# A two-layer decoder kernel: another PSUM bank for one tile, high passes of a pair ahead of low ones, and weight splits of two units at other steps

## What is computed

```python
h = rms_norm(x, norm_w[i])
proj = h @ w_in                      # layer 0: q, kc, vc, ks, vs, kw, vw, gates, z
# layer 0: rope on q, ks, kw; compressed, selected and window branches
o = g0 * o_cmp + g1 * o_sel + g2 * o_win
x = x + (o * silu(z)) @ w_out
# layer 1: q, f, i, z = split(h @ w_in); chunkwise gated recurrence
o = o * rsqrt(mean(o * o) + eps)     # per head, then g_norm
x = x + (o * silu(z)) @ w_out
```

## Time and profile before

| | us |
|---|---|
| median of 3 runs | 330.6 |
| lowest and highest | 330.0, 330.66 |
| the profiled execution | 330.72 |
| its span, first to last instruction | 328.9 |

### The profile page before, as it was taken

How to read it: one execution, slowest core, us unless ns; L and a number is a source line. 1 busy time by engine, 2 the same in 40 slices (tenths; PEclk the granted TensorE clock), 3 DMA queues, 4 the chain that set the end, 5 groups by cost and what they waited for, 6 DMA issues and landing times.

```text
span 328.9 us, 6172 instructions
## 1 busy us (share of the span) xinstructions
PE 317.3 (96%) x2380; PEld 268.4 (82%) x2380; DVE 228.9 (70%) x400; ACT 188.6 (57%) x400; POOL 57.8 (18%) x55
## 2 busy tenths in 40 slices
PE   7999999999999999999999999999999999998993
PEld 5889778867989877777678878999999788897882
DVE  2789953649569978879828726277449988489824
ACT  4694355356696666668536706838345036898223
POOL 1004022070423443346300010100000011101000
PEclk9999999999999999999999999999999999999998
DMA  7999999806390920033270773653662424001011
GB/s 229 394 335 209 265 358 195 264 31 223 105 186 0 212 47 2 0 112 146 68 253 0 257 258 127 248 201 91 227 249 91 168 96 165 2 1 66 0 64 64
DMA packets 28828, 49.41 MB, mean 150 GB/s; under 512 B 3256, under 2 KB 7744, under 8 KB 28800
## 3 DMA queue, kind: packets, MB, share of 16 engines
q1 hardware_dynamic: 25760, 44.30, 42.9%
q10 hardware_dynamic: 2528, 2.69, 4.2%
q0 software_dynamic: 512, 2.03, 1.9%
HBM read 47.97 MB, written 1.05 MB: 149 GB/s over the span
## 4 chain that ended last, share of the span: by engine, by line
PE 66%; DVE 16%; ACT 5%; issue 2%; POOL 2%; ACTq 0%; DVEq 0%; POOLq 0%
PE bank L548 61%; DVE w_lo L1073 6%; ACT w_hi L826 3%; PE bank L727 3%; DVE nmax L1268 2%; POOL rp L1427 1%; PE bank L648 1%; DVE prob_t L1280 1%; DVE qk L1357 1%; DVE ft L1324 1%; DVE qk L1343 1%; PE bank L592 1%; DVE zT L1215 1%; DVE zT L1216 0%; ACT prob L946 0%
## 5 line engine op out<-in xcount | busy, mean ns | idle before, releaser
L1073 DVE TENSOR_TENSOR w_lo<-raw,w_hi 128x1024 fp32r<-128x1024 f32 (+1 forms) x80 | 89.2, 1159 | 34.8 <-ACT w_hi L826 34.7
L548 PE MATMUL bank<-w_hi,h_hi 128*128 128x512 f32 x192 | 77.9, 412 | 2.4 <-DVE h_lo L1172 1.1
L548 PE MATMUL bank<-w_hi,h_lo 128*128 128x512 f32 x192 | 75.2, 392 | 0.0
L548 PE MATMUL bank<-w_lo,h_hi 128*128 128x512 f32 x192 | 75.2, 392 | 0.0
L826 ACT ACTIVATE w_hi<-raw 128x1024 fp32r<-128x1024 f32 (+1 forms) x80 | 72.9, 967 | 2.1 <-issue 1.9
L548 PE MATMUL bank<-h_hi,w_hi 128*128 128x256 f32 x224 | 64.9, 290 | 0.1
L548 PE MATMUL bank<-h_hi,w_lo 128*128 128x256 f32 x224 | 63.5, 283 | 0.0
L548 PE MATMUL bank<-h_lo,w_hi 128*128 128x256 f32 x224 | 63.5, 283 | 0.0
L548 PEld LDWEIGHTS bank<-w_hi,h_hi 128*128 128x128 f32 x192 | 35.9, 188 | 11.4 <-issue 4.0
L548 PEld LDWEIGHTS bank<-h_hi,w_hi 128*128 128x128 f32 x224 | 43.0, 192 | 0.5 <-DVE w_lo L1073 0.3
L548 PEld LDWEIGHTS bank<-h_lo,w_hi 128*128 128x128 f32 x224 | 43.0, 192 | 0.3
(11 more groups left out here) (194 smaller groups left out, 424.3 us busy)
## 6 DMA issues: line engine op xcount, KB each, us to landing
raw<-in_hg SPq DMA_DIRECT2D x16, 1024.0 KB, 7.4
raw<-in_nsa SPq DMA_DIRECT2D x12, 1024.0 KB, 9.0
raw<-in_nsa_out SPq DMA_DIRECT2D x8, 512.0 KB, 8.5
raw<-in_hg_out SPq DMA_DIRECT2D x4, 1024.0 KB, 6.2
raw<-in_nsa SPq DMA_DIRECT2D x8, 256.0 KB, 5.9
w<-in_w1k SPq DMA_DIRECT2D x2, 1024.0 KB, 16.3
w<-in_w1v ACTq DMA_DIRECT2D x2, 1024.0 KB, 15.8
x_res<-in_x SPq DMA_DIRECT2D x4, 256.0 KB, 5.2
```

The costliest lines, as they stand in the source:

```text
L548: return nc.tensor.matmul(o, lhsT, rhs, start=start, stop=stop, skip_group_check=True)
L1073: m = V.tensor_tensor(lo, src, hi.bitcast(F32), ALU.subtract)
```

## The change

Four edits. (1) The first tile of the third unit, (U_KW, 0), goes to PSUM bank 7 instead of 0. (2) In every "pa" step but those of the first unit, the two high passes of the pair stand ahead, and wait for `hi_done` alone; the low passes behind them wait for `lo_done`. (3) SPREAD of U_Q1 is (10, 12, 13, 13) instead of (10, 13, 20, 26). (4) SPREAD of V_O0 is (0, 1, 5, 5) instead of (0, 3, 2, 2).

```diff
-        "E": [(("pa", U_KW, 0, sl), 0) for sl in range(4)],
+        "E": [(("pa", U_KW, 0, sl), 7) for sl in range(4)],
...
-SPREAD = {... U_Q1: (10, 13, 20, 26), ... V_O0: (0, 3, 2, 2), ...}
+SPREAD = {... U_Q1: (10, 12, 13, 13), ... V_O0: (0, 1, 5, 5), ...}
...
-                    for kk in (2 * sl, 2 * sl + 1):
+                    two = (2 * sl, 2 * sl + 1)
+                    hi = [h_hi[:, kk, t * P:(t + 1) * P] for kk in two]
+                    for j, kk in enumerate(two):
+                        pe.wait_ge(hi_done, split_count(u, kk))
+                        mm(ps[:], hi[j], w_hi[:, u % 2, kk], kk == 0, False)
+                    for j, kk in enumerate(two):
                         parts(u, kk)
-                        hi = h_hi[:, kk, t * P:(t + 1) * P]
-                        mm(ps[:], hi, w_hi[:, u % 2, kk], kk == 0, False)
-                        mm(ps[:], hi, w_lo[:, u % 2, kk], False, False)
+                        mm(ps[:], hi[j], w_lo[:, u % 2, kk], False, False)
                         m = mm(ps[:], h_lo[:, kk, t * P:(t + 1) * P], w_hi[:, u % 2, kk], False, kk == KT - 1)
```

More of the change, by code:

```diff
@@ L214, in split_count @@
     return kk + 1 if u == 0 else KT + NQ * (u - 1) + kk // 2 + 1
-SPREAD = {U_KW: (6, 7, 7, 0), U_Q0: (9, 5, 18, 15), U_Q1: (10, 13, 20, 26), U_Z0: (4, 0, 7, 12), U_Z1: (6, 7, 8, 12), U_O0: (17, 14, 28, 45), U_O1: (31, 47, 66, 93), V_V0: (0, 0, 1, 4), V_V1: (0, 0, 3, 6), V_F0: (0, 0, 11, 0), V_Q0: (2, 7, 20, 19), V_F1: (3, 5, 5, 6), V_Q1: (1, 0, 4, 9), V_Z0: (3, 5, 3, 5), V_Z1: (4, 0, 44, 39), V_O0: (0, 3, 2, 2), V_O1: (3, 1, 7, 4)}
+SPREAD = {U_KW: (6, 7, 7, 0), U_Q0: (9, 5, 18, 15), U_Q1: (10, 12, 13, 13), U_Z0: (4, 0, 7, 12), U_Z1: (6, 7, 8, 12), U_O0: (17, 14, 28, 45), U_O1: (31, 47, 66, 93), V_V0: (0, 0, 1, 4), V_V1: (0, 0, 3, 6), V_F0: (0, 0, 11, 0), V_Q0: (2, 7, 20, 19), V_F1: (3, 5, 5, 6), V_Q1: (1, 0, 4, 9), V_Z0: (3, 5, 3, 5), V_Z1: (4, 0, 44, 39), V_O0: (0, 1, 5, 5), V_O1: (3, 1, 7, 4)}
 GATED_LAG = 3
```

## The result

The changed kernel takes 331.49 us (median of 9 runs, 331.11 to 333.48) where the kernel before takes 330.52 (9 runs, 330.00 to 330.66). The medians are 0.97 us apart (0.29%), against a forecast of +1.05 and 331.65 us. The ratio over all runs, which lies near that of the means (331.98 and 330.48), is 1.0047, 95% interval 1.0028 to 1.0066. One thing wasn't in the forecast: the changed kernel's executions form two groups, five at 331.11 to 331.49 with a mean granted TensorE clock of 0.996 to 0.998, and four at 332.50 to 333.48 with 0.992 or 0.993. The profiled one is of the second group (332.5 us, span 330.7, clock 0.993).

What follows compares the result with a forecast made beforehand. TensorE, busy 317.3 of 328.9 us, was taken as the bound, leaving little but its waits to win. Terms -0.15 + 1.55 - 0.35 = +1.05 us on 330.72, less 0.12 to the median, gave 331.65 us; range 329.8 to 332.8.

Steps and rivals of the forecast that it cites:

- U_Q1, +1.55 forecast: Second query unit: quarter 1's w_lo, now ahead of the rotary work, makes TensorE 1.55 us later at the stage transposes.
- the 0.3 of a short one: At U_Q1: with GpSimd's sum priced at 1.29 us instead of 2.19, a loss of only 0.3 us.
- twice in line: Rival at U_Q1: GpSimd's sum waits for both w_lo, the copy starts 1.15 later; 332.8 us, chance 0.10.
- U_KW, -0.15 forecast: Third unit's first tile: high passes going first gain 0.46 us, of which waiting for the w1k transfer leaves 0.15.
- The prediction's sign of error: At the first compression matmul: a start at 40.1, not about 40.4, would show the forecast wrong.
- The bank 0: At U_KW's first tile: the other PSUM bank by itself gives 0.
- the 176 waits 0: In 88 pair steps: two more TensorE waits each cost nothing; at 10 ns each they would be 1.8 us.
- V_O0, -0.35 forecast: First output unit: new splits gain 0.99 us at its first pass, much given back later, leaving 0.35 gained.
- The wait of about 0.2 forecast ahead of V_O0: Ahead of the first output unit: a TensorE wait of about 0.2 us would show the forecast right.
- Aim reached: Rival: the wait at 74.73 goes and nothing else is late, needing rotary work by about 69.1; 329.2 us, chance 0.17.

Runs made afterwards that it cites:

- e1: The changed kernel with the splits of U_Q1 back at their old steps (10, 13, 20, 26): 330.00 us, ratio 0.9980 to the kernel before.
- e10: The changed kernel plus only 4 fill matmuls, ahead of the stage transposes, leaving the 1.68 us stop: 332.22 us, ratio 1.0047 to the kernel before.
- e8: The kernel before with only the first tile of U_KW moved to bank 7 from 0: 330.65 us, ratio 0.9998.
- e5: The kernel before with the new pair order alone, old bank and all old splits: 330.45 us, ratio 1.0000.
- e6: The kernel before with the splits of V_O0 at (0, 1, 5, 5) alone: 330.67 us, ratio 1.0004.
- e3: The changed kernel with a lag of 2 instead of 1 for U_Q1, its first w_lo again behind the rotary work: 329.06 us, ratio 0.9953.
- e2: The kernel before with the new splits of U_Q1 (10, 12, 13, 13) alone: 333.34 us, ratio 1.0077.
- e9: The changed kernel plus only 14 fill matmuls, ahead of the second kv's transposes, leaving the 0.63 us stop: 331.39 us, ratio 1.0026.

## Why the prediction was right, and where it was not

- **U_Q1, +1.55 forecast, +1.34 measured.** In the forecast's clock (after's rows plus 0.80): rotary work 70.54 (forecast 70.55), sum 72.14 and 2.18 long (72.17 and 2.19), stg copy 74.42 (74.45), hid 74.96 (74.99), transposes 75.42 (75.45). Only the last step was mis-sized: GpSimd's second step was to be held by the w_lo of quarter 3 until 75.5. The pair of w_lo ended at 71.18 + 3.43 = 74.61, 75.41 in that clock, but the step was only 0.12 longer than before (1.41 for 1.29, from 75.13), so the stage transposes came at 76.68 and not at 76.9. The sum's long price was right; the 0.3 of a short one is excluded.
- **The clock, not forecast.** The prediction followed each wait to its end and then let TensorE run on at its full pace. That a stop of 0.93 grown to 1.68 us has a price of its own was missed. It is some 1.4 us, as much as the term itself, in four of nine executions. That the forecast held all the same is luck in part: had the clock fallen in one more of the nine, the median would have been about 332.5, outside its 331.3 to 332.3. The rival "twice in line" (332.8) named the time of the slower group (332.67), but by a mechanism that didn't occur: GpSimd's sum never waited for both w_lo.
- **U_KW, -0.15 forecast.** The profiled execution shows -0.44; nine profiles give -0.14 on average. The mechanism is as forecast, 0.53 gained (forecast 0.46) and then capped by the transfer of w1k, but the size moves from 0.51 to -0.41 with the landing, so the near hit of the mean is luck. The start some 0.1 behind the landing that the forecast took (40.4 for 40.3) has no row of its own; in the six profiles with a wait it came out at 0.08 to 0.19. The prediction's sign of error, a compression matmul at 40.1, was met: at 40.10 in e1 and 40.01 in e10, and in the changed kernel's own execution at 39.76 (40.12 with the 0.36 of chance taken off). It says that the transfer landed early there, not that the order failed.
- **The bank 0, the 176 waits 0.** Both right as far as the runs can tell (e8; e5 at 1.0000, and its passes are 0.23 us apart).
- **V_O0, -0.35 forecast, -0.37 measured (1.02 less 0.65), by its own steps.** These rows answer to the earlier trace rows, 2.03 late by the offset at 286 us, and TensorE's first w_lo pass of V_O1 at 307.75 - 2.03 = 305.72 was forecast for 305.75:

```profile
302.64 0.69 DVE L1367 TENSOR_REDUCE ostat<-fg 128x4 f32<-128x512 f32 x1 [1.57 <-ACT fg L1004]
...
306.47 2.35 DVE L1076 TENSOR_TENSOR w_lo<-raw,w_hi 128x1024 fp32r<-128x1024 f32 x2
...
312.34 1.28 DVE L1175 TENSOR_TENSOR h_lo<-bank,h_hi 128x512 fp32r<-128x512 f32 x2
```

  The wait of about 0.2 forecast ahead of V_O0 isn't there: the row at 301.34 has no bracket, since the recurrence's matmuls ran until then. What wasn't said is that this term belongs to two parts of the change: without the new pair order it is zero (e6).
- **The sum.** -0.14 + 1.34 - 0.37 = +0.83, against 331.31 - 330.52 = +0.79 in the executions whose clock held. The median of 331.49 is the uppermost of these, and so lies nearer to 331.65 than the terms deserve: luck again.
- **Aim reached** was given 0.17 at 329.2, on the condition that the rotary work starts by 69.1. It didn't come about: the rotary work started at 69.74, 70.54 in the forecast's clock. e3, another kernel, meets the condition by the order alone (67.68) and takes 329.06, so the rival was well priced, and the aim of the new splits is reached once that w_lo is out of the way.

## What to carry to other kernels

Where a split is put forward, ask on each engine apart what it gets ahead of: the high parts were free on ScalarE, and the low part, which could not begin before its high part was done, held VectorE's whole queue. Where a wait is made longer on an engine that is otherwise dense, price the stretch behind it at both clocks, and look at the single executions, not the median alone, for a second group. A gain at one place is worth only what the next waiting step lets through, so measure parts together and apart: order and splits showed no gain alone (ratios 1.0000 and 1.0004), and 0.12% together.

## What the runs showed of the hardware

TensorE's granted clock fell from 2.4 to 1.2 GHz from about 77 to 80 us (76.8 to 80.1 in the changed kernel, 77.3 to 80.7 in e2), shortly after it had stood idle for 1.68 and 0.63 us, in some executions and not in others of the same kernel. It came back with work going on. No time or clock of the 11 runs of e9, with a stop of 0.63 us alone, shows such a fall, nor one of the 93 runs of the kernel before and e1, with one of 0.93 to 0.98 us here; a stop of 1.12 or 1.13 ahead of V_O0 left the clock at 1.00 in the four profiles that have it (before, e2, e5, e8). Eighteen matmuls whose result nobody reads, in the place of the idle time, kept the clock up and cost nothing that the runs can tell (331.41 against 331.31 us).

A GpSimd sum of 128x512 took 2.18 to 2.32 us where VectorE ran a w_lo beside it, and 1.28 where it did not. VectorE's two w_lo took 3.43 us together beside it, and 2.35 elsewhere.
